# Neighbourhood attention: query blocks of 8 rows by 16 columns and bands of 12 rows by 32 columns in place of 2-row blocks with bands of whole rows

## The reference, cut to what matters

```python
c0 = jnp.clip(cols - kc // 2, 0, GRID_W - kc)            # kc = 16
col_bias = rpb[:, :, col_idx - cols[:, None] + NA_WIN_COLS - 1]
def row_block(r):
    r0 = jnp.clip(r - kr // 2, 0, rows - kr)             # kr = 8
    s_win = einsum('bhqd,bhrqcd->bhqrc', q_r, k_win) * scale + bias
    s_ctx = einsum('bhqd,bkhd->bhqk', q_r, k_ctx) * scale
    p = softmax(concatenate([s_win, s_ctx], axis=-1))
    return p_win @ v_win + p_ctx @ v_ctx
```

## Time and profile before

| | us |
|---|---|
| median of 3 runs | 3208.7 (3206.51 to 3210.6) |
| the profiled execution | 3206.72 |
| its span, first to last instruction | 3204.9 |
| TensorE busy | 3017.3 (94%) |
| DVE, ACT, POOL busy | 1761.0, 814.2, 737.9 |
| mean granted TensorE clock | 0.978 |

### The profile page before, as it was taken

How to read it: one execution, slowest core, us unless ns; L and a number is a source line. 1 busy time by engine, 2 the same in 40 slices (tenths; PEclk the granted TensorE clock), 3 DMA queues, 4 the chain that set the end, 5 groups by cost and what they waited for, 6 DMA issues and landing times.

```text
span 3204.9 us, 44556 instructions
## 1 busy us (share of the span) xinstructions
PE 3017.3 (94%) x15712; PEld 2495.8 (78%) x15712; DVE 1761.0 (55%) x2975; ACT 814.2 (25%) x1412; POOL 737.9 (23%) x457
## 2 busy tenths in 40 slices
PE   6899999799999999999979899999798999999997
PEld 2688887478888888888669788888676888888884
DVE  1645545667766667654551366666614555555456
ACT  1411111321111111111142366656613111111111
POOL 0311111021111111111111344545421222222220
PEclk8999999899999999999989899999999999999998
DMA  9110103022122222111035556555630111111111
GB/s 357 71 53 26 52 26 88 0 69 79 54 79 69 74 79 66 61 40 39 33 105 126 160 155 177 164 145 142 192 121 27 39 58 40 45 53 39 59 39 59
DMA packets 156872, 269.26 MB, mean 84 GB/s; under 512 B 70272, under 2 KB 97920, under 8 KB 156800
## 3 DMA queue, kind: packets, MB, share of 16 engines
q1 hardware_dynamic: 156800, 268.32, 26.6%
HBM read 222.13 MB, written 50.07 MB: 85 GB/s over the span
## 4 chain that ended last, share of the span: by engine, by line
PE 77%; DVE 6%; issue 6%; DMA 4%; ACT 3%; POOL 2%; SPq 1%; DVEq 0%; POOLq 0%; ACTq 0%
PE psum L653 41%; PE psum L682 19%; PE psum L807 4%; PE psum L787 3%; PE psum L628 2%; PE psum L861 2%; PE psum L830 2%; PE psum L844 2%; DVE residual L1307 1%; DMA o_dram<-o_st_lo 1%; DVE prod L1287 1%; POOL w_lo L1621 1%; DMA mod_raw<-mod_panels 1%; ACT pt_hi L1124 1%; PE psum L740 1%
## 5 line engine op out<-in xcount | busy, mean ns | idle before, releaser
L1307 DVE SCALAR_TENSOR_TENSOR residual<-psum,modulation,residual 128x512 f32<-128x512 f32 (+1 forms) x1072 | 718.0, 689 | 890.4 <-PE psum L682 888.7
L1621 POOL TENSOR_TENSOR w_lo<-raw,w_hi 128x1024 fp32r<-128x1024 f32 x196 | 491.2, 2519 | 1929.8 <-ACT w_hi L951 1926.1
L653 PE MATMUL psum<-act_hi,w_hi 128*128 128x512 f32 (+1 forms) x2208 | 589.6, 367 | 9.6 <-POOL w_lo L1621 7.6
L653 PE MATMUL psum<-act_lo,w_hi 128*128 128x512 f32 (+1 forms) x2208 | 589.0, 367 | 0.0
L653 PE MATMUL psum<-act_hi,w_lo 128*128 128x512 f32 (+1 forms) x2208 | 588.7, 367 | 0.0
L653 PEld LDWEIGHTS psum<-act_hi,w_hi 128*128 128x128 f32 x2208 | 397.8, 188 | 88.4 <-issue 7.8
L951 ACT ACTIVATE w_hi<-raw 128x1024 fp32r<-128x1024 f32 x196 | 204.1, 1060 | 1018.7 <-PE psum L653 945.0
L682 PE MATMUL psum<-prod_hi,w_hi 128*128 128x512 f32 (+1 forms) x1072 | 408.6, 381 | 28.5 <-DVE residual L1307 11.1
L653 PEld LDWEIGHTS psum<-act_lo,w_hi 128*128 128x128 f32 x2208 | 380.2, 188 | 70.7
L653 PEld LDWEIGHTS psum<-act_hi,w_lo 128*128 128x128 f32 x2208 | 380.2, 188 | 70.5
L682 PE MATMUL psum<-prod_hi,w_lo 128*128 128x512 f32 (+1 forms) x1072 | 396.2, 370 | 0.0
(11 more groups left out here) (117 smaller groups left out, 3780.8 us busy)
## 6 DMA issues: line engine op xcount, KB each, us to landing
raw<-ffn_panels SPq DMA_DIRECT2D x132, 512.0 KB, 5.0
mod_raw<-mod_panels SPq DMA_DIRECT2D x48, 512.0 KB, 9.5
mod_in<-mod_rest SPq DMA_DIRECT2D x64, 384.0 KB, 3.1
raw<-conv_panels SPq DMA_DIRECT2D x32, 512.0 KB, 5.2
k_hi<-k_dram SPq DMA_DIRECT2D x32, 320.0 KB, 5.7
k_lo<-k_dram SPq DMA_DIRECT2D x32, 320.0 KB, 7.3
v_st<-v_dram SPq DMA_DIRECT2D x32, 320.0 KB, 7.1
raw<-qk_panels SPq DMA_DIRECT2D x16, 512.0 KB, 4.7
```

The source lines that it names most:

```text
L653: mm = pe.matmul(psum[:, bank + b, 0:tn], w[:, s, kb, :], acts[h][:, kb, t0:t0 + tn], start=(kb == 0 and n == 0), stop=(kb == KB - 1 and n ...
L1307: dve.scalar_tensor_tensor(out=residual[:, ob, t0:t0 + tn], in0=psum[:, 6 + r % 2, 0:tn], scalar=modulation[:, gates + ob, kind_of(t0):kin ...
L1621: pool.tensor_tensor(panel(w_lo, s), raw[:, s], panel(w_hi, s), ALU.subtract).then_inc(lo_done[s], 1)
```

## The change

Queries are laid out in column blocks. A unit is now one block of 16 columns and all 16 rows, its halves `ab` are the upper and lower 8 rows, 128 queries each. The band of keys of a half is 12 rows by 32 columns, 384 keys, the same shape for every unit; PE reads it from the same `k_hi` and `k_lo` as 12 runs of 32 numbers. The two halves share two of the four 128-key tiles (4 rows by 32 columns) of a column block; the other tiles belong to one half alone, so that `values` has four tiles of 256 columns and two of 128. A unit has three groups always, 24 a pair where there were 28. The scale goes to the keys and not the queries; ACT and DVE write query tiles in the new order, `store_o` writes 128 numbers a run, and the sum behind the output projection turns the order back with four DVE instructions of 128 columns where one of 512 was (`L1568` before).

Values have to lie with the 128 keys of a tile on partitions: `load_v` gathers them with 16 DMAs of 32 partitions and one for the context, a head, and they exist once for each of the four overlapping column windows. The bias is finished beforehand: for each head, half and kind of column block (first, inner, last) a table of 128 queries by 384 keys in DRAM with the mask in it. 96 DMAs fill it with the mask value during the convolution, and during the last four steps of the first FFN 6 stages of 16 loads of bias rows, an addition of the mask on POOL and 16 stores write the rest. `load_bias` reads six tables a head in place of one. `tables` goes from POOL, the 32 copies go from SP.

```diff
-        GROUPS = [OUTER, INNER, INNER, OUTER]
+        SLOTS_OF = [[(0, 1, ((0, BAND + P), (1, BAND))), (2 * P, 2, ((0, BAND + 2 * P), (1, BAND + P)))],
+                    [(4 * P, "c0", ((0, C0), (1, C0))), (6 * P, "c1", ((0, C1), (1, C1)))],
+                    [(8 * P, 0, ((0, BAND),)), (9 * P, 3, ((1, BAND + 2 * P),))]]
+        GROUPS = len(SLOTS_OF)
         UNITS = 8
...
-        QK_CHUNKS = {**chunks(1, 2, 0, (5, 5, 5, 5, 4)), **chunks(1, 3, 6, (6, 6, 6, 6)), **chunks(1, 4, 11, (8, 8, 8)),
-                     **chunks(2, 0, 15, (5, 5, 5, 5, 4)), **chunks(2, 1, 21, (5, 5, 5, 5, 4))}
-        QK_DRAINED = {6: (1, 2), 11: (1, 3), 15: (1, 4), 21: (2, 0), 27: (2, 1)}
+        QK_CHUNKS = {**chunks(1, 2, 0, (8, 8, 8)), **chunks(1, 3, 4, (8, 8, 8)), **chunks(1, 4, 8, (12, 12)),
+                     **chunks(2, 0, 11, (6, 6, 6, 6)), **chunks(2, 1, 16, (5, 5, 5, 5, 4))}
...
+            def fill_tables(j):
+                for h in range(HEADS // KB):
+                    for ab in range(2):
+                        for kind in range(COL_KINDS):
+                            sp.dma_start(bias_dram[j * (HEADS // KB) + h, ab, kind],
+                                         bias_stage[0][:, 0:BAND_ROWS]).then_inc(bias_filled, 16)
+
+            sp.wait_ge(consts, CONSTS)
+            fill_tables(0)
...
+            def load_bias_rows(n):
+                group, kind = divmod(n, COL_KINDS)
+                at_least(sp, bias_out, 16 * ROWS * (n - 1))
+                for c in range(Q_COLS):
+                    src = bass.AP(tensor=rpb_padded.tensor,
+                                  offset=group * HEAD_GROUP * REL * PADW + GRID_W - 1 - kind * Q_COLS // 2 - c,
+                                  ap=[[REL * PADW, HEAD_GROUP], [PADW, REL], [1, WINDOW]])
+                    sp.dma_start(bias_stage[n % 2][c * HEAD_GROUP:(c + 1) * HEAD_GROUP, EDGE:EDGE + REL],
+                                 src).then_inc(bias_in[n % 2], 16)
+
+            def store_bias_rows(n):
+                group, kind = divmod(n, COL_KINDS)
+                table = P * BAND_KEYS
+                sp.wait_ge(bias_masked, n + 1)
+                for row in range(ROWS):
+                    ab, r = divmod(row, WIN_ROWS)
+                    first = min(max(row - EDGE, 0), ROWS - WIN_ROWS)
+                    begin = EDGE + first - row + WIN_ROWS - 1
+                    offset = ((group * HEAD_GROUP * 2 + ab) * COL_KINDS + kind) * table
+                    offset += (r * Q_COLS * BAND_ROWS + first - EDGE * ab) * WINDOW
+                    dst = bass.AP(tensor=bias_dram[:].tensor, offset=offset,
+                                  ap=[[BAND_KEYS, Q_COLS], [2 * COL_KINDS * table, HEAD_GROUP], [1, WIN_ROWS * WINDOW]])
+                    sp.dma_start(dst, bias_stage[n % 2][:, begin:begin + WIN_ROWS].rearrange("p r k -> p (r k)")
+                                 ).then_inc(bias_out, 16)
...
-            with sp.Fori(MOD_GROUPS + 2, HIDDEN) as j:
+            for j in range(MOD_GROUPS + 2, HIDDEN):
                 load_ffn0(j)
+                n = 2 * (j - MOD_GROUPS - 2)
+                for k in (n - 2, n - 1):
+                    if 0 <= k < BIAS_STAGES:
+                        store_bias_rows(k)
+                    if k + 2 < BIAS_STAGES:
+                        load_bias_rows(k + 2)
             sp.wait_ge(rest_acc, GROUP_STEPS * MOD_GROUPS)
...
             def load_bias(i, b):
                 at_least(sp, s_done, 16 * i + 8 * b - 8)
-                sp.dma_start(bias_full[0:GRID_W, b, 1:REL], bias_dram[2 * i + b, :, 1:REL]).then_inc(bias_rows_in[b], 16)
-                sp.dma_start(bias_full[GRID_W:P, b, 1:REL], bias_dram[2 * i + b, :, 0:REL - 1]).then_inc(bias_rows_in[b], 16)
+                for ab in range(2):
+                    for kind in range(COL_KINDS):
+                        sp.dma_start(bias[b][ab][kind][:], bias_dram[2 * i + b, ab, kind]).then_inc(bias_rows_in[b], 16)
 
             def load_heads(i, b):
                 sp.wait_ge(qk_out, 32 * NQK * (i + 1))
...
             def load_v(i, b):
                 at_least(sp, pv_ready, 8 * i + 4 * b - 4)
-                for part in range(2):
-                    tiles = slice(part * TOK_TILES // 2, (part + 1) * TOK_TILES // 2)
-                    sp.dma_start(v_st[:, b, tiles].bitcast(F32),
-                                 v_dram[2 * i + b, :, tiles].rearrange("p t n d -> p t (n d)")).then_inc(v_in[b], 16)
+                row = 2 * DH
+                head = (2 * i + b) * T * row
+                for j in range(COL_BLOCKS):
+                    for r in range(KEY_ROWS):
+                        src = bass.AP(tensor=v_dram[:].tensor, offset=head + (r * GRID_W + WINDOWS[j]) * row,
+                                      ap=[[row, WINDOW], [KEY_ROWS * GRID_W * row, ROW_TILES], [1, row]])
+                        dst = v_st[b][r * WINDOW:(r + 1) * WINDOW, j * ROW_TILES:(j + 1) * ROW_TILES]
+                        sp.dma_start(dst.bitcast(F32), src).then_inc(v_in[b], 16)
+                src = bass.AP(tensor=v_dram[:].tensor, offset=head + TL * row, ap=[[row, P], [P * row, CTX_TILES], [1, row]])
...
             def store_o(i, u):
-                h0, q0 = DH * (u // 4), 4 * (u % 4) * GRID_W
+                h0 = DH * (u // 4)
                 sp.wait_ge(o_lo_done, UNITS * i + u + 1)
                 for dram, stage in zip(o_dram, (o_st_hi, o_st_lo)):
-                    sp.dma_start(dram[i, h0:h0 + DH, q0:q0 + 2 * P], stage[h0:h0 + DH, :]).then_inc(o_out, 16)
+                    dst = dram[i, h0:h0 + DH, :].rearrange("p (n j q) -> p n j q", n=2, j=COL_BLOCKS)
+                    sp.dma_start(dst[:, :, u % 4], stage[h0:h0 + DH, :].rearrange("p (n q) -> p n q", n=2)
+                                 ).then_inc(o_out, 16)
 
...
-                rest = rows * GRID_W - TC
-                for bank, col, key, n in ((0, 0, TL, TC), (0, TC, k0, TC), (1, 0, k0 + TC, rest)):
-                    for part, k in enumerate((k_hi, k_lo)):
-                        mm = pe.matmul(psum[:, 2 * ab + bank, col:col + n], q_st[:, b, q0:q0 + P],
-                                       k[:, b, key:key + n], start=(part == 0), stop=(part == 1))
+                j = u % 4
+                q0 = ab * BANK + j * P
+                for part, k in enumerate((k_hi, k_lo)):
+                    rows = k[:, b, 0:TL].rearrange("p (r c) -> p r c", c=GRID_W)
+                    pe.matmul(psum[:, 2 * ab, 0:BAND_KEYS], q_st[:, b, q0:q0 + P],
+                              rows[:, EDGE * ab:EDGE * ab + BAND_ROWS, WINDOWS[j]:WINDOWS[j] + WINDOW],
+                              start=(part == 0), stop=(part == 1))
+                for part, k in enumerate((k_hi, k_lo)):
+                    mm = pe.matmul(psum[:, 2 * ab + 1, 0:TC], q_st[:, b, q0:q0 + P], k[:, b, TL:T],
+                                   start=(part == 0), stop=(part == 1))
...
-                                             in1=residual[:, p, t0:t0 + tn], op0=ALU.mult,
-                                             op1=ALU.add).then_inc(y_added, 1)
+                    for j in range(COL_BLOCKS):
+                        rows = by_column_block(residual[:, p, t0:t0 + tn])[:, j]
+                        blocks = as_column_blocks(psum[:, 6 * (p % 2) + b, 0:tn])
+                        dve.scalar_tensor_tensor(out=rows, in0=blocks[:, j],
+                                                 scalar=modulation[:, MODS + 2 * KB + p, 0:1], in1=rows,
+                                                 op0=ALU.mult, op1=ALU.add).then_inc(y_blocks, 1)
+                    dve.wait_ge(y_blocks, COL_BLOCKS * (len(LAT) * p + b + 1))
+                    dve.sem_inc(y_added, 1)
...
+            with pool.Fori(0, MOD_GROUPS + 2) as j:
                 ffn_step("ffn0", j)
+            for j in range(MOD_GROUPS + 2, HIDDEN):
+                ffn_step("ffn0", j)
+                for n in range(2 * (j - MOD_GROUPS - 2), 2 * (j - MOD_GROUPS - 1)):
+                    if n < BIAS_STAGES:
+                        mask_bias_rows(n)
             norm(2, ALL)
```

More of the change, by code:

```diff
@@ L840, in turn @@
                 col = 0
-                for slot, _, starts in GROUPS[u % 4][g]:
-                    for ab, start in enumerate(starts):
-                        if start is not None:
-                            mm = pe.transpose(psum[:, 4 + (group0[u] + g) % 2, col:col + P],
-                                              probs[:, 2 * (u % 2) + ab, start:start + P], ident[:])
-                            col += P
+                for _, _, starts in SLOTS_OF[g]:
+                    for ab, start in starts:
+                        mm = pe.transpose(psum[:, 4 + (group0[u] + g) % 2, col:col + P],
+                                          probs[:, 2 * (u % 2) + ab, start:start + P], ident[:])
+                        col += P
                 mm.then_inc(pt_ready, 1)
@@ new lines, in _ @@
+            first, inner, last = (col_mask[:, kind, :] for kind in range(COL_KINDS))
```

(11 more changed lines are left out.)

230 lines of the change are left out of this document (101 added, 129 removed).

## The result

The changed kernel takes 3318.7 us (median of 4 runs, 3317.5 to 3323.8), the kernel before 3207.6: ratio 1.0349, 95% interval 1.0335 to 1.0363. The profiled execution has a span of 3315.6 us, 110.7 more than the 3204.9 of before.

A forecast was written before the change was run, and what follows sets the result against it. PE was taken to set attention's pace, with SP's queue the unseen resource the change loads. 3206.7 + 47 + 25 + 4 - 2 + 10 + 1 = 3291.7, said as 3290 us; range 3200 to 3370.

The forecast's parts named there:

- first FFN, last steps: Steps 19 and 20: 64 small DMAs on SP delay the next panels, PE stands still 21 us twice; +47 us.
- to the first panels of attention: Start of attention: first stores of queries and keys wait behind twelve table loads, next queries behind 17 value loads; +10 us.
- pairs 0 to 5: Attention: output 4 goes out 18 us after output 3 and PE stalls; 70 us a pair for 65.85, +25 us.
- pairs 6 and 7: Last attention pairs: pair 6 +4 us with `o_hi` loads behind its block, pair 7 -2 us.
- The fills: 96 fills during the convolution hold SP 4 to 5 us a step, covered by a later wait; cost nothing.
- Price of a value gather: SP's time for a 32-partition value load in attention, taken as 0.62 us from copies on 64 partitions.
- The high bound of 78: Attention, pairs 0 to 5, with dearer SP issues: 78 us a pair, +73 us; printed for 0.89 us an issue.
- PE's gain: Attention: PE's counted work falls from 62.0 to 54.0 us a pair, 8.0 less.
- the reads in runs of 32 numbers: Rival, attention scores: PE reads them slower, 0.30 rather than 0.17, 4 us a pair, within +15; no chance given.
- Cheap issues: Rival: all small copies on SP at 0.37 us, decided below about 0.41; total 3194 us, chance 0.12.
- Dear issues: Rival: SP's issues as dear as the 15-row copy; FFN +74, pairs +73, total 3376 us, chance 0.20.
- One queue only: Rival: only FFN or only attention is hurt by SP's queue; 3262 or 3245 us, chance 0.20.

The follow-up runs named there:

- e4: Changed kernel with attention's same DMAs in another order on SP, values, tables and heads spread between outputs: 3222.9 us, ratio 1.0045.
- e9: Changed kernel with bias copies moved, attention DMAs reordered and staging halved (3175.1 us), plus next head's queries and latent keys loaded behind output 2: 3167.6 us.
- e6: Changed kernel without the bias table loads after those of pair 0 (output differs): 3262.1 us, ratio 1.0172.
- e3: Changed kernel with the output's staging in two halves of partitions by the unit's parity, a semaphore for each: 3255.9 us, ratio 1.0152.
- e1: Changed kernel with one set of 32 FFN bias copies a step instead of two, the last four sets behind the values' weights: 3276.7 us, ratio 1.0218.

## Why the prediction was right, and which terms were off

The side and the two places were right, and the time (3290 forecast, 3318.7 measured) was 29 us short. The profiled spans, cut at the same marks (ACT's first split behind the FFN's last step, SP's first panels of attention, its panels ahead of pair 6, the last output's store), give the terms:

| stage | forecast | measured |
|---|---|---|
| first FFN, last steps | +47 | +41.9 |
| to the first panels of attention | +10 | +6.9 |
| pairs 0 to 5 | +25 | +56.3 (pair 0 +5.0, the others 329.2 to 380.5) |
| pairs 6 and 7 | +2 | +8.0 |
| after them (cause not looked for) | +1 | -2.3 |
| sum | +85 | +110.7 |

**FFN.** Right in mechanism and nearly in size. From one issue to the next a load takes 0.72 us (11.44 / 16) and a store 0.64, 0.68 on the mean for the 0.65 taken; the lag of the stores was 1.8. SP issued the next panels 55.8 us after the step's start for 54.1 forecast, and the first was split 3.6 later for 5.0, so that two errors met. ACT waited 39.8 and 37.8 us for the panel and PE 20.0 and 17.9 for its low part, 21 forecast; the clock was 0.50 in the gap (12 us from 1494 on) and 0.60 in the 6 us from 1507 on. The waits of PE make 37.9 of the 41.6 us; the other 3.7 fit the low clock, 5 forecast.

**The fills** cost nothing, as forecast: the FFN step that began at 1444.93 before begins at 1445.18.

**Price of a value gather.** Taken as 0.62; the row says 0.317 for the instruction itself, but 0.50 from one to the next (2058.68, 2059.18, 2059.68 in the chain). The text, and the section on time and profile before it, took the length of a row for the time that the instruction holds the queue; the distance between two is longer. The same holds for the tables: 0.346 and 0.52. The values of a block took 8.7 us for 10.5, the rest of it (output 3, queries, keys, tables) 8.8 for 7.5: that the sum came out at 17.5 for 18 is in part luck. The text named gathers under 0.45 us as proof of a wrong forecast, and by the row's length it was met; it was badly put, since the forecast needs the distance. (The high bound of 78 goes with 0.86 us, not with the 0.89 printed.)

**PE's gain.** Forecast 62.0 to 54.0 a pair. At full clock a pair takes PE 63.4 us before (mean of pairs 1 to 5) and 55.4 to 55.6 in e4 and e9: the count lies some 1.5 low on both sides, and the gain, 7.9, is the 8.0 forecast. One row of it was off: the values on 128 columns take about 0.11 us from start to start, as much as on 256 columns, and not 0.09 (PE in the changed kernel, 256 and 128 columns):

```profile
2068.06 0.28 PE L925 MATMUL psum<-pt_hi,v_second 128*128 128x256 f32 x1
2068.18 0.28 PE L925 MATMUL psum<-pt_lo,v_second 128*128 128x256 f32 x1
...
2069.72 0.28 PE L925 MATMUL psum<-pt_lo,v_second 128*128 128x128 f32 x1
2069.83 0.28 PE L925 MATMUL psum<-pt_hi,v_second 128*128 128x128 f32 x1
2069.94 0.28 PE L925 MATMUL psum<-pt_lo,v_second 128*128 128x128 f32 x1
```

The 384-column scores take 0.175, and the reads in runs of 32 numbers cost nothing: that rival is out. In the changed kernel itself PE's busy time fell by 15.5 us only, not 60: a pair's instructions, 55.5 us at full clock, took 61.1 at a clock of 0.89 to 0.91.

**The step that was mis-sized: a pair's stall, +4.2 forecast, +10.3 measured in pairs 1 to 5.** Output 4's late issue was right (17.5 us behind output 3). Three things around it were not.

- *Before it.* Output 3 goes out 39.9 to 41.5 us after the pair's start, forecast 37. The text names both waits there, behind the value loads and behind the tables ahead of the keys' store, and gives them 1.6 us on PE (and 2 more for the value block at the pair's end); ACT's rows have 4.32 and 4.93, and PE idled 4.76 for the second.
- *Behind it.* The text has one wait of ACT a pair, until output 4 lands; there is a second of 5 to 6 us for output 5. Its store is issued behind the 1.8 MB of the next head and lands in 6.3 us instead of 2.0. It did so in the kernel before, but there ACT came to the next unit 8.8 us after the last one (1931.14, 1939.90), and now it is ready 4.4 us after (2071.68, 2076.12). From the landing of output 4 to the pair's end it takes 14.9 us, forecast 12.
- *The clock.* Forecast 2 us a pair; the 61.1 for 55.5 above are 5.6, a part of them inside waits.

e6 gives 57 us back, by its rows about three quarters of it time that SP needs to issue the tables. e3 shows the tie through which all of these waits are felt: with a second half of staging 63 come back. The Trainium skill (DMA: Bandwidth & Descriptors, Two DMAs through the same engine are not ordered) says that within one queue of one engine descriptors start in order; a store of 2.0 us that takes 6.3 behind loads agrees.

**The rivals.** Cheap issues (below 0.41) is refuted: the distances are 0.48 to 0.72. Dear issues (3376) is refuted as to its price, though a pair took nearly its 78. One queue only (3262 or 3245) is refuted by e1 and e4, which give back 42 and 96 us.

## What to carry to other kernels

Price a queue by the distance from one issue to the next, not by the length of an issue. Then follow every small store that something waits for: when it can be issued, how many bytes stand right before it (behind 1.8 MB it landed in 6.3 us, although the DMA engines' mean share was 0.65), and when its buffer is wanted. A late landing that cost nothing before costs as soon as the work comes faster. When a change cuts compute and adds small transfers, spread them over the gaps between those stores before giving it up: here their order, with a second half of staging and a loop written out, turned 3.5% slower into 1.4% faster than before. Where one staging buffer waits for such a store, look for an unused half of it.
